# A first mix with its eight heads in pairs: row and column halves of the array, softmax sums spread by TensorE, new engine orders

## The reference, cut to what matters

```python
h = rms_norm(x, norm1_g[l])
proj = h @ w_in[l]
q, k, v, u = jnp.split(proj, [512, 1024, 1536], axis=-1)       # 8 heads of 64
q = apply_rope(rms_norm(q, q_norm_g[l]), cos, sin)
k = apply_rope(rms_norm(k, k_norm_g[l]), cos, sin)
attn = softmax(causal(q @ k.T * 64 ** -0.5)) @ v                # 256 tokens are one block
a, g = jnp.split(u + glu_b, 2, axis=-1)
c = a * jax.nn.sigmoid(g)                                       # 512 channels
c = causal_depthwise_conv(c, dw_w) + dw_b                       # 31 taps
conv = jax.nn.silu(layer_norm(c, ln_g, ln_b))
x = x + jnp.concatenate([attn, conv], axis=-1) @ w_out[l]
```

## Time and profile before

| | us |
|---|---|
| median of 3 runs | 1297.12 (1296.93 to 1297.52) |
| the profiled execution, its own time | 1296.65 |
| its span in the trace | 1294.8 |
| busy: TensorE, VectorE, ScalarE, GpSimd | 1284.3, 840.7, 677.7, 121.4 |
| granted TensorE clock, mean | 0.999 of 2.4 GHz |

### The profile page before, as it was taken

The page is one execution under the profiler, slowest core; times in us unless marked ns, Lnnn a source line. Parts: engine busy times, 40 slices in busy tenths (PEclk is TensorE's granted clock), DMA queues, the critical chain, the costliest instruction groups (busy, mean ns, idle before and its releaser), DMA issues.

```text
span 1294.8 us, 18327 instructions
## 1 busy us (share of the span) xinstructions
PE 1284.3 (99%) x7086; PEld 1103.0 (85%) x7086; DVE 840.7 (65%) x1098; ACT 677.7 (52%) x903; POOL 121.4 (9%) x137
## 2 busy tenths in 40 slices
PE   8999999999999999999999999999999999999998
PEld 7988888888888888888888888888888877888886
DVE  7997755565655548897765556665555677665552
ACT  6866554444544436656554445444454665564441
POOL 4860000000000001012100000000001120000000
PEclk9999999999999999999999999999999999999999
DMA  9425765563765544426565554675554655465540
GB/s 293 158 82 181 249 221 195 194 206 122 240 202 190 191 137 136 148 107 199 198 221 195 194 195 143 215 255 186 186 189 131 214 191 164 150 226 185 185 150 33
DMA packets 174351, 234.96 MB, mean 181 GB/s; under 512 B 4351, under 2 KB 154127, under 8 KB 174288
## 3 DMA queue, kind: packets, MB, share of 16 engines
q1 hardware_dynamic: 170368, 223.52, 52.4%
q0 software_dynamic: 3184, 9.37, 2.3%
q10 hardware_dynamic: 736, 1.19, 0.3%
HBM read 233.03 MB, written 1.05 MB: 181 GB/s over the span
## 4 chain that ended last, share of the span: by engine, by line
PE 98%; DVE 1%; ACT 0%; DMA 0%; issue 0%; POOL 0%; DVEq 0%; SPq 0%; ACTq 0%
PE psum L1213 22%; PE psum L1108 16%; PE psum L1110 15%; PE psum L1109 15%; PE psum L1221 12%; PE psum L1234 2%; PE psum L1176 2%; PE psum L1175 2%; PE psum L1174 2%; PE psum L1238 1%; PE psum L1334 1%; PE psum L1459 1%; PE psum L1446 1%; PE psum L1436 0%; PE psum L1410 0%; PE psum L1135 0%
## 5 line engine op out<-in xcount | busy, mean ns | idle before, releaser
L1852 DVE TENSOR_TENSOR w_lo<-raw,w_hi 128x2048 fp32r<-128x2048 f32 (+1 forms) x199 | 456.8, 2301 | 84.6 <-ACT w_hi L470 83.1
L470 ACT ACTIVATE w_hi<-raw 128x2048 fp32r<-128x2048 f32 (+1 forms) x212 | 403.2, 1906 | 34.1 <-PE psum L1110 13.7
L1213 PE MATMUL psum<-t_both,w_hi 128*128 128x512 f32 x1280 | 304.7, 390 | 0.0
L1213 PEld LDWEIGHTS psum<-t_both,w_hi 128*128 128x128 f32 x1280 | 237.4, 188 | 47.4
L1108 PE MATMUL psum<-w_hi,f_hi 128*128 128x512 f32 x488 | 192.7, 395 | 0.0
L1110 PE MATMUL psum<-w_hi,f_lo 128*128 128x512 f32 x488 | 190.2, 390 | 0.0
L1109 PE MATMUL psum<-w_lo,f_hi 128*128 128x512 f32 x488 | 190.1, 389 | 0.0
L1108 PE MATMUL psum<-w_hi,t_both 128*128 128x512 f32 (+2 forms) x464 | 166.5, 359 | 0.2
L1110 PE MATMUL psum<-w_hi,t_both 128*128 128x512 f32 (+2 forms) x464 | 162.4, 350 | 0.0
L1109 PE MATMUL psum<-w_lo,t_both 128*128 128x512 f32 (+2 forms) x464 | 162.2, 349 | 0.0
L1221 PEld LDWEIGHTS psum<-t_both,w_lo 128*128 128x128 f32 x1280 | 158.9, 192 | 3.1
(11 more groups left out here) (230 smaller groups left out, 1342.3 us busy)
## 6 DMA issues: line engine op xcount, KB each, us to landing
raw<-in_ffn_wg SPq DMA_DIRECT2D x44, 1024.0 KB, 5.6
raw<-in_ffn_wu SPq DMA_DIRECT2D x44, 1024.0 KB, 5.4
raw<-in_ffn_wd SPq DMA_DIRECT2D x44, 1024.0 KB, 5.0
raw<-in_even_w_in SPq DMA_DIRECT2D x12, 1024.0 KB, 5.2
raw<-in_odd_w_in SPq DMA_DIRECT2D x12, 1024.0 KB, 5.2
raw<-in_w_gate SPq DMA_DIRECT2D x11, 1024.0 KB, 5.5
raw<-in_w_up SPq DMA_DIRECT2D x11, 1024.0 KB, 5.4
raw<-in_w_down SPq DMA_DIRECT2D x11, 1024.0 KB, 5.0
```

The costliest lines, as they stand in the source:

```text
L470: nc.scalar.activation(w_hi[:, n % SLOTS, 0:w], raw[:, n % RAWS, 0:w], ACT.Copy).then_inc(hi_done, 1)
L1213: mm = nc.tensor.matmul(bank[b + c][:, :], wh[:, k, c * P:(c + 1) * P], t_both[:, k, :, :].rearrange("p a s -> p (a s)"), start=k == 0 and ...
L1852: nc.vector.tensor_tensor(w_lo[:, n % SLOTS, 0:w], raw[:, n % RAWS, 0:w], w_hi[:, n % SLOTS, 0:w].bitcast(F32), ALU.subtract).then_inc(lo_ ...
```

## The change

Scores, values, sums and orders of the first mix change; nothing else does.

- The scores of heads h and h + 1 are issued together by `pair_scores`, rows 0 to 63 and 64 to 127 by turns. The even head's go to bank 4, the odd one's to bank 3 (heads 0 to 3) or bank 0 (heads 4 to 7). So the first piece of the convolution, which writes bank 3, waits for the maxima of head 3; the scores of head 4 wait until bank 0 is read; and the first `rows` wait for the maxima of head 7.
- The values of two heads are issued together by `pair_values`, the output now with channels on the partitions, 64 columns of the array for each head. `group_turn` is gone.
- The sums are no longer applied with tokens on the partitions. VectorE takes the reciprocals of a group (`group_sums`), TensorE spreads them over 64 partitions each by matmuls of a broadcast column with the identity (`group_spread`, eight fp32 matmuls of 128 columns in column halves), ScalarE copies the bank to SBUF (`keep_sums`), and VectorE multiplies the output in its bank by it (`group_scale`). `group_hi` waits for that.
- Tap 27 of channel tile 2 goes from VectorE's list to TensorE's last piece, which has four taps now.
- The lists of all four engines in the first mix are ordered anew. VectorE splits unit 10 in front of the maxima of heads 2 and 3, and unit 11 in front of those of heads 4 and 5; before, unit 11 stood in front of head 6. The second group's scale stands behind `side_ok`, the low part of group 1 behind the centring.

```diff
-                         sq=g_row.rearrange("p (c s) -> p c s", c=4), o=[wv(7032 + 512 * g, T, 256) for g in range(2)],
+                         sq=g_row.rearrange("p (c s) -> p c s", c=4), inv=[wv(7032 + 512 * g, 512) for g in range(2)],
...
-                V["L"]["row_scale"] = row_scale
+                V["L"].update(row_scale=row_scale, s_bank=lambda h: bank[4 if h % 2 == 0 else 3 if h < 4 else 0])
...
-        PE_TAPS = {ACT_PE: range(20, TAPS), DVE_PE: range(28, TAPS)}
+        PE_TAPS = {ACT_PE: range(20, TAPS), DVE_PE: range(27, TAPS)}
...
+            def keep_sums(b, inv):
+                act.wait_ge(sums_T, nx(sums_T))
+                nc.scalar.activation(inv, bank[b][:, :], ACT.Copy).then_inc(sums_kept, 1)
...
                 taps(2)
+                exps(L, 1)
                 keep_rope(units[6][3], 7)
                 keep_pt(L, 0)
-                exps(L, 1)
-                taps(2)
+                taps(1)
                 square(8)
                 keep_pt(L, 1)
+                taps(1)
                 exps(L, 2)
+                exps(L, 3)
+                taps(1)
+                keep_pt(L, 2)
+                taps(2)
+                keep_unit(ph, 9)
+                keep_rope(units[8][3], 7)
+                keep_pt(L, 3)
                 taps(3)
-                keep_pt(L, 2)
-                exps(L, 3)
-                keep_rope(units[8][3], 7)
+                exps(L, 4)
+                exps(L, 5)
+                keep_pt(L, 4)
+                keep_sums(1, V["inv"][0])
                 taps(1)
-                keep_unit(ph, 9)
-                taps(2)
-                keep_pt(L, 3)
-                exps(L, 4)
-                taps(2)
-                keep_pt(L, 4)
-                exps(L, 5)
-                group_hi(0, 6)
+                group_hi(0, 6, scaled=True)
+                taps(1)
+                exps(L, 6)
                 keep_pt(L, 5)
-                exps(L, 6)
+                exps(L, 7)
                 keep_pt(L, 6)
-                exps(L, 7)
                 keep_pt(L, 7)
                 split_to(12)
-                group_hi(1, 7)
+                keep_sums(5, V["inv"][1])
+                group_hi(1, 7, scaled=True)
                 split_to(13)
...
+            def group_hi(g, b, L=None, scaled=False):
 
                 if L:
                     act.wait_ge(o_done, L["h0"] + 4 * g + 4)
+                elif scaled:
+                    act.wait_ge(o_scaled, nx(o_scaled))
                 else:
                     act.wait_ge(o_T, nx(o_T))
...
-                    add(5)
+                    add(3)
                     build(1)
                     add(2)
                     build(1)
+                    add(2)
...
+            def pair_values(L, h, out):
 
                 pe.wait_ge(pt_kept, L["h0"] + h + 2)
                 for kt in range(2):
                     for c in range(2):
-                        mm = nc.tensor.matmul(out[64 * c:64 * c + 64, P * kt:S], v[:, kt, 64 * (h + c):64 * (h + c) + 64],
+                        mm = nc.tensor.matmul(out[64 * c:64 * c + 64, P * kt:S], L["v"](h + c, kt)[:, 0:64],
                                               pt_buf[:, c, 2 * P * kt:2 * P * kt + S - P * kt], start=kt == 0, stop=kt == 1)
                         if kt:
                             mm.then_inc(o_done, 1)
...
+            def group_spread(L, lo, b):
+
+                pe.wait_ge(sums_ok, nx(sums_ok))
+                for pair in range(2):
+                    for t in range(T):
+                        for c in range(2):
+                            at = 2 * (lo + 2 * pair + c) + t
+                            mm = nc.tensor.matmul(bank[b][64 * c:64 * c + 64, pair * S + t * P:pair * S + (t + 1) * P],
+                                                     L["sum"][:, at:at + 1].broadcast_to([P, 64]), ident[:, :], start=True, stop=True)
+                mm.then_inc(sums_T, 1)
...
                     pe.wait_ge(rope_kept, 2 if h < 4 else 4)
-                    head_scores(L, h)
+                    if h == 4:
+                        pe.wait_ge(bank_free[0], left[8])
+                    pair_scores(L, h)
...
-                    head_values(L, h)
+                    at = h % 4 // 2 * S
+                    pair_values(L, h, bank[6 + h // 4][:, at:at + S])
...
+                    if p == 0:
+                        pe.wait_ge(nmax_ok, L["h0"] + 4)
...
+                    if i == 7:
+                        scores(0)
+                    if i == 8:
+                        turn(0)
+                    if i == 9:
+                        turn(1)
+                        scores(2)
+                    if i == 10:
+                        values(0)
+                        turn(2)
+                    if i == 11:
+                        turn(3)
+                    if i == 12:
+                        values(2)
+                        scores(4)
                     if i == 13:
-                        group_turn(V["o"][0], 6)
-                    if 7 <= i < 15 and i != 11:
-                        scores(i - 7)
-                    if 8 <= i:
-                        turn(i - 8)
-                    if 9 <= i:
-                        values(i - 9)
-                    if i == 11:
-                        scores(4)
-                pe.wait_ge(bank_free[0], left[8])
-                pe.wait_ge(bank_free[1], left[9])
+                        turn(4)
+                        pe.wait_ge(bank_free[1], left[9])
+                        group_spread(L, 0, 1)
+                    if i == 14:
+                        scores(6)
+                        turn(5)
+                    if i == 15:
+                        values(4)
+                        turn(6)
+                pe.wait_ge(nmax_ok, L["h0"] + 8)
                 rows(0, 0, (0,))
-                values(7)
+                turn(7)
                 rows(0, 0, (1,))
-                group_turn(V["o"][1], 7)
+                values(6)
+                group_spread(L, 4, 5)
                 pe.wait_ge(conv_ok, 2)
                 pe.wait_ge(side_ok, 1)
-                pe.wait_ge(nmax_ok, L["h0"] + 8)
...
                 taps(2)
                 rooted_maxima(0)
                 rope_end(6)
+                rooted_maxima(1)
                 taps(5)
-                rooted_maxima(1)
                 split_to(10)
-                taps(4)
                 rooted_maxima(2)
+                rooted_maxima(3)
                 taps(3)
                 mean_square(3)
                 rope_begin(8)
                 taps(2)
-                rooted_maxima(3)
                 rope_end(8)
-                taps(10)
+                split_to(11)
+                taps(5)
+                group_sums(L, 0)
                 rooted_maxima(4)
-                taps(5)
                 rooted_maxima(5)
-                taps(1)
-                group_out(L, 0, V["o"][0], 6)
-                split_to(11)
+                taps(6)
+                group_scale(L, 4, 6, V["inv"][0])
+                taps(2)
                 rooted_maxima(6)
+                rooted_maxima(7)
                 group_lo(0, 6)
                 taps(5)
-                rooted_maxima(7)
-                taps(TAPS)
-                group_out(L, 1, V["o"][1], 7)
+                group_sums(L, 4)
+                taps(PE_TAPS[DVE_PE].start + TAPS)
                 dve.wait_ge(conv_ok, 2)
                 dve.wait_ge(piece_done, len(PIECES))
                 dve.wait_ge(tap_added, TAPS - 1)
                 nc.vector.tensor_tensor(V["acc"][:, 2:4, :], bank[3][:, :].rearrange("p (a s) -> p a s", a=2), V["acc"][:, 2:4, :], ALU.add)\
                     .then_inc(side_ok, 1)
-                group_lo(1, 7)
+                group_scale(L, 8, 7, V["inv"][1])
                 dve.wait_ge(mean_ok, 1)
                 nc.vector.tensor_tensor(V["acc"], V["acc"], bank[4][:, 0:S].unsqueeze(1).broadcast_to([P, 4, S]), ALU.subtract)\
                     .then_inc(cen_ok, 1)
+                group_lo(1, 7)
                 split_to(12)
                 dve.wait_ge(var_ok, 1)
...
+            def group_sums(L, lo):
+
+                dve.wait_ge(p_done, 2 * (L["h0"] + lo + 4))
+                v = L["sum"][:, 2 * lo:2 * lo + 8]
+                nc.vector.reciprocal(v, v).then_inc(sums_ok, 1)
+
+            def group_scale(L, hi, b, inv):
+
+                dve.wait_ge(o_done, L["h0"] + hi)
+                dve.wait_ge(sums_kept, nx(sums_kept))
+                nc.vector.tensor_tensor(bank[b][:, :], bank[b][:, :], inv, ALU.mult).then_inc(o_scaled, 1)
```

More of the change, by code:

```diff
@@ L258, in build @@
         p_mixed = sem("p_mixed")
+        sums_ok = sem("sums_ok")
+        sums_T = sem("sums_T")
+        sums_kept = sem("sums_kept")
+        o_scaled = sem("o_scaled")
         hi_done = sem("hi_done")
@@ L886, in mix_even @@
                 group_hi(3, 7)
-            def group_hi(g, b, L=None):
+            def group_hi(g, b, L=None, scaled=False):
                 if L:
```

(6 more changed lines are left out.)

## The result

| | before | changed |
|---|---|---|
| median of 22 runs, us | 1296.91 (1296.18 to 1297.58) | 1298.99 (1296.73 to 1299.52) |
| the profiled execution: its time, its span | 1296.65, 1294.8 | 1298.84, 1297.0 |

The ratio is 1.0014, with a 95% interval of 1.0008 to 1.0020: the change made the kernel slower by 2 us, a little inside the 0.2% that I had called "no change", and outside my range of 1293.7 to 1297.6. Of the 22 runs of the changed kernel, 2 lie at 1296.73 and 1296.85, at the time of the kernel before, with a mean clock of 1.000; 16 lie between 1298.7 and 1299.5 and 4 between the two groups, all 20 with a mean clock of 0.998 or less. A single mean would hide that.

The account below looks back on a forecast made before the run. TensorE and VectorE, reaching the channel mean within 0.16 us of each other, bound it together. TensorE's -3.9 us mostly becomes waiting; VectorE's 2.17 less 1.2 gives 1.0 earlier, 1296.1 against the median 1297.12; range 1293.7 to 1297.6.

Parts of the forecast that it names:

- VectorE's gain of 1.0 us in front of the mean: VectorE's last convolution sum before the channel mean: 2.17 us saved less 1.2 us of new waits, so 1.0 earlier.
- TensorE in front of the mean: TensorE's work before the channel mean: scores -3.4, values and group turns -2.0 and -, spreads +1.1, tap +0.45; sum -3.9 us.
- six entries at 0.09: TensorE's six entries into column halves: at 0.09 us each the saving would be 0.5 us smaller, the mean's start unmoved.
- new waits, 1.2 us: VectorE before the mean: waits at maxima 2, 4, 6 and the first scale, 0.4 to 0.5, 0.3, 0.3, 0.1 us.
- My walk: Step-by-step timing of VectorE's new list against TensorE up to the mean, giving 1.2 us of new waits.
- 0.1 for ScalarE: TensorE's turn 4, in front of the first spread: it may wait 0.1 us for ScalarE.
- before 88, against 96 needed: GpSimd's last two additions, behind one more build: they end before 88 us, against 96 needed.
- The pause: TensorE, ready near 93.3, waits about 2.7 us for VectorE in front of the mean, which starts near 96.2.
- Rival 3: TensorE's clock falls in the new pause before the mean, costing 1.7 to 4 us; time 1299; chance 0.07.
- Behind the mean: After the mean every queue keeps its order, and nothing more is added or lost.
- The low part of group 1: VectorE, between centring and unit 12: 0.61 us covered by 0.99 us idle before the variance, 0.4 left.
- rival 2: VectorE before the mean: new waits of 2.2 us take all the gain; time 1297.1, no change; a fifth of 0.75.

Follow-up runs that it names:

- experiment 3: Changed kernel with VectorE's taps moved in front of its three large waits, same work in all: 1296.25 us, ratio 0.9993 to the kernel before.
- experiment 7: Changed kernel with VectorE's order of experiment 3 and another ScalarE order (copy of head 5 earlier, one tap product later): 1294.93 us, ratio 0.9982.
- experiment 5: Kernel before, with four PSUM bank copies added on VectorE in front of its last convolution sum: 1301.67 us, ratio 1.0035.
- experiment 6: Kernel before, with six PSUM bank copies added on VectorE in front of its last convolution sum: 1303.95 us, ratio 1.0055.
- experiment 1: Changed kernel with eleven idle fp32 matmuls on TensorE between the second spread and the wait before the mean: 1297.25 us, ratio 0.9999.
- experiment 4: Changed kernel with VectorE's order of experiment 3 and one ScalarE tap product moved behind exponentials 4: 1295.49 us, ratio 0.9988.
- experiment 8: Kernel of experiment 7 with three more fp32 matmuls between the two halves of the variance's one-column matmuls: 1294.42 us, ratio 0.9980.
- experiment 2: Changed kernel with taps 23 to 26 of channel tile 2 left out of VectorE's list: 1295.37 us, ratio 0.9984.

## Why the prediction was wrong, point by point

Two steps failed, and together they make all but 0.2 of the 2.9 us between 1296.1 and 1298.99: VectorE's gain of 1.0 us in front of the mean came out at 0.1, and the fall of the clock, 1.8 us, was left out of the sum.

**TensorE in front of the mean: right.** Scores 0.86 (0.85 forecast), values 0.80 (0.80), spread 1.03 (1.0). From the first scores to the mean, without waits, TensorE needed 34.36 us (59.17 to 94.81 less 1.28) instead of 38.12 (58.72 to 97.24 less a wait of 0.40): 3.76 less, where the sum says 3.9. It was ready at 94.8 where I had 93.3. Of the 1.5 us between, 0.9 are waits (1.06 and 0.22, against the 0.40 that the kernel before had at the same turn) and 0.45 is the later start of this execution. The halves of the spread do run side by side. The Trainium skill (TensorEngine Tiling (Array Packing), Key Properties) says that a change of tiling mode drains TensorE. With six entries at 0.09 the sum was to be 0.5 smaller; it came out 0.14 smaller, too little to decide anything.

**VectorE's gain in front of the mean: wrong, the term "new waits, 1.2 us".** They were 3.85. Two of the four were mis-sized for a reason that cost little: I let GpSimd slow the splits of units 10 and 11 (2.96 and 2.73), and it did not; they took 2.33 and 2.28, so VectorE was at the maxima sooner and waited longer, 1.32 instead of 0.5 and 0.91 instead of 0.3. The next wait ended when TensorE ended it. The third is the real miss: the first scale waited 1.37, not 0.1. My walk put the spread on TensorE at once behind turn 4 and gave turn 4 "0.1 for ScalarE". ScalarE had three tap products in front of exponentials 4, and each of its tap products waits for GpSimd's addition of the tap two before:

```profile
77.66 0.91 ACT L715 ACTIVATE ws<-ws,tap_col 128x256 f32<-128x256 f32 x2 [0.96 <-POOL ws L1039]
79.09 0.91 ACT L715 ACTIVATE ws<-ws,tap_col 128x256 f32<-128x256 f32 x2 [0.52 <-POOL ws L1039]
80.50 0.91 ACT L715 ACTIVATE ws<-ws,tap_col 128x256 f32<-128x256 f32 x2 [0.50 <-POOL ws L1039]
81.31 0.39 ACT L685 ACTIVATE ws<-ws,st 128x128 f32<-128x128 f32 x1
```

Those rows are ScalarE in the changed kernel: 2 us of waits in front of exponentials 4, a chain from GpSimd over ScalarE and TensorE to VectorE. I had costed GpSimd only at its end ("before 88, against 96 needed"), not at what its additions hold up on the way.

The first of these waits, 0.96, begins on VectorE itself. The interference that I had booked on the splits had not gone, it had changed sides. One addition of GpSimd, in the changed kernel, and in the kernels of experiments 3 and 7:

```profile
74.51 3.12 POOL L1039 TENSOR_TENSOR ws<-ws 128x512 f32<-128x512 f32 x1
75.22 1.86 POOL L1039 TENSOR_TENSOR ws<-ws 128x512 f32<-128x512 f32 x1
75.22 2.55 POOL L1039 TENSOR_TENSOR ws<-ws 128x512 f32<-128x512 f32 x1
```

Undisturbed such an addition takes 1.27 us. In each of the three it began while VectorE split unit 11 (from 74.21, 73.66 and 74.36 on) and ended 1.1 us behind the split's end. In the kernel before the addition began first, at 83.88, and took 1.29; there the split took the longer time, 2.73. The wait follows: where the addition was held for 1.9 or 1.3 us, ScalarE's first tap product waited 0.96 and 0.97 and turn 4 waited 1.06 and 1.07; where it was held for 0.6, they waited 0.27 and 0.38. Experiments 3 and 7 have the same lists up to turn 4, so no order that was tried takes this away, and its size changes from execution to execution; that the early place of unit 11 makes it is read from traces, and no run moves that split alone. The whole chain did not have to cost anything: with VectorE's taps in front of its waits (experiment 3) VectorE has none of its four waits left in front of the last sum, and in experiment 7, where turn 4 waited 1.07 again, the first scale had no wait either.

**The pause: right in place, size and price, and wrong in its chance.** I forecast 2.7 us of TensorE idle in front of the mean; it was 2.79. (From its own 93.3 and 96.2 the forecast would be 2.9.) That the size fits so well is luck: TensorE was ready 1.5 us later than forecast and VectorE 1.4, in good part by the same wait at turn 4. Rival 3 named the fall of the clock there, gave it 1.7 to 4 us, and the cost was 1.8. Its time of 1299 is met by luck too: it puts 3 us for the clock on top of VectorE's gain of 1.0, and neither was so. The failed step is the chance, and with it a sum without the clock: I gave it 0.07, arguing that "this pause has full work on both sides". Experiments 5 and 6 show that full work on both sides is no protection, and by the times and mean clocks of the 22 runs it struck in 16 to 20 of them. My own forecast needed a pause longer than the one of 2.4 us that I had read from the end of the kernel, so rival 3 was a consequence of the forecast and not a case beside it. The Trainium skill (TensorE: Matmul & The Clock Gate, HAM oscillation) warns of idle gaps in a matmul kernel for this reason. The runs agree with its direction; the gaps that it names are longer than this one, and here 2.72 and 2.79 us were enough.

**Behind the mean: right in order.** The low part of group 1 cost nothing (0.43 us of idle left before the variance where I had 0.4, and 0.41 in experiment 1 with the clock up), and the second scale ran under the mean.

With the clock at its upper level (two runs) the changed kernel is at 1296.8, between my forecast of 1296.1 and no change; rival 2 (the waits take all) is what happened there.

## What to carry to other kernels

A saving on the busiest engine is worth what the engine it next meets lets it keep: find that meeting point, and take work from both sides of it or from neither. A pause on TensorE is not only idle time; where the forecast opens one like the 2.7 us of this case, its price includes the clock (0.7 us did not bring the fall in the one trace that has it), and idle matmuls in it cost next to nothing here. When a list is reordered into pairs, look at what each engine does in front of the hand-over, and also at what a slow third engine holds up in the middle of its list, not only at where it ends.

## What the runs showed that I had not expected

The clock also falls without a long pause. Behind sixteen matmul records of one column, in which the profile calls TensorE busy, the stretch from 102.6 to 106.0 in the trace of experiment 4 has a granted clock of 0.50, the lower level, with TensorE busy through all of it. With three filler matmuls of 128 columns among them (0.75 us from start to start) the mean clock was 0.999 or more in 11 of 11 runs of experiment 8, against 6 of 11 without them in experiment 7.

What exactly brings this fall stays open. The same sixteen records stand in the kernel before (from 101.72), in the changed kernel, and in the traces of experiments 1, 2, 3 and 7, and the clock behind them is 1.00 in all six; a wait of 0.22 us stood in front of them in experiment 4, and one of 0.21 in experiment 3, where nothing fell. So they are no cause by themselves. The runs of the upper groups in experiments 3 and 7 were not traced either, so that they are this fall is an inference from one trace and from experiment 8.
